# Rebuilding the routing chain between mixer and experts, and moving the mixers' scratch out of the weight slots

## The reference

```python
for l in range(DEPTH):                      # DEPTH = 2
    hn = rms_norm(x, norm_mix[l])
    mix = even_mixer(...) if l % 2 == 0 else odd_mixer(...)
    x = x + mix
    x = x + hier_moe(rms_norm(x, norm_ffn[l]), ...)
...
g_logits = xt @ w_group + b_group           # 4 groups
e_logits = xt @ w_expert + b_expert         # 32 experts
e_sel = the 8 logits of the best group;  top_v, top_i = top_k(e_sel, 2)
gate = softmax weights of the two experts * probability of the group
for each expert: acc += ge * ((silu(xt @ w1) * (xt @ w3)) @ w2)
```

## Time and profile before

| | |
|---|---|
| device time, median of 3 runs (us) | 1127.63 (1126.7 to 1129.67) |
| profiled execution: its time / its span (us) | 1127.25 / 1125.4 |
| mean granted TensorE clock | 0.956 of full speed |
| busy: PE, PEld, DVE, ACT | 76%, 48%, 32%, 23% |
| moved by DMA | 442.95 MB, mean 394 GB/s |
| layer 0: mixer and routing / experts from | 0 to 160 us / 160 us |
| layer 1: mixer and routing / experts from | 584 to 691 us / 691 us |

### The profile page before, as it was taken

The page is one execution under the profiler, slowest core; times in us unless marked ns, Lnnn a source line. Parts: engine busy times, 40 slices in busy tenths (PEclk is TensorE's granted clock), DMA queues, the critical chain, the costliest instruction groups (busy, mean ns, idle before and its releaser), DMA issues.

```text
span 1125.4 us, 25604 instructions
## 1 busy us (share of the span) xinstructions
PE 856.0 (76%) x10392; PEld 542.8 (48%) x10393; DVE 354.9 (32%) x841; ACT 262.3 (23%) x502; POOL 7.5 (1%) x16
## 2 busy tenths in 40 slices
PE   9999997777766666666689998777766666666665
...
GB/s 357 254 166 169 378 349 417 427 430 430 433 430 430 432 433 431 430 432 432 431 416 342 208 429 388 418 420 429 434 430 431 431 432 430 431 434 430 431 430 259
DMA packets 50189, 442.95 MB, mean 394 GB/s; under 512 B 4320, under 2 KB 5792, under 8 KB 23648
## 3 DMA queue, kind: packets, MB, share of 16 engines
...
q10 hardware_dynamic: 144, 0.52, 0.1%
q0 software_dynamic: 128, 0.26, 0.1%
...
## 4 chain that ended last, share of the span: by engine, by line
DMA 47%; PE 39%; DVE 6%; ACT 4%; issue 3%; SPq 1%; ACTq 0%; DVEq 0%
DMA up_pairs<-in_moe_w_dram 44%; PE low_banks L1280 13%; PE low_banks L1298 4%; PE sums_of_x L831 3%; PE sums_of_x L832 3%; PE sums_of_x L833 3%; DMA weights<-in_moe_w_dram 3%; PE low_banks L1256 2%; PE low_banks L831 1%; PE sums_of_x L1309 1%; PE low_banks L833 1%; PE low_banks L832 1%; PE low_banks L1047 1%; PE sums_of_x L1312 1%; DVE w_lo L1755 1%
## 5 line engine op out<-in xcount | busy, mean ns | idle before, releaser
L1280 PE MATMUL low_banks<-up_pairs,gates 128*32 128x256 f32 x4096 | 273.4, 426 | 117.1 <-DMA up_pairs<-in_moe_w_dram 103.4
L1280 PEld LDWEIGHTS low_banks<-up_pairs,gates 128*32 128x32 f32 x4096 | 140.7, 122 | 234.1 <-DMA up_pairs<-in_moe_w_dram 113.3
L1298 PE MATMUL low_banks<-weights,gates 128*32 128x256 f32 x2016 | 122.3, 382 | 83.0 <-DVE gates L2177 52.5
L2175 DVE TENSOR_TENSOR gates<-gates,low_banks 128x128 f32<-128x128 f32 x64 | 18.4, 287 | 389.8 <-ACT gates L1344 389.8
L1298 PEld LDWEIGHTS low_banks<-weights,gates 128*32 128x32 f32 x2016 | 62.6, 109 | 142.2 <-issue 80.8
L1344 ACT ACTIVATE gates<-low_banks 128x128 f32<-128x128 f32 x64 | 17.8, 278 | 406.4 <-PE low_banks L1280 406.4
L2171 DVE TENSOR_TENSOR gates<-low_banks,vecs 128x256 f32<-128x256 f32 x64 | 27.2, 424 | 260.6 <-PE low_banks L1265 260.6
L1256 PE MATMUL low_banks<-y_T,gates 128*32 128x256 f32 x1024 | 68.5, 385 | 13.9 <-issue 9.4
L1755 DVE TENSOR_TENSOR w_lo<-weights,w_hi 128x2048 fp32r<-128x2048 f32 x28 | 64.0, 2287 | 14.7 <-ACT w_hi L1415 14.5
L1586 ACT COPY gates<-low_banks 128x256 f32<-128x256 f32 x64 | 23.8, 372 | 191.2 <-PE low_banks L1298 191.2
L1580 ACT COPY gates<-low_banks 128x256 f32<-128x256 f32 x64 | 23.8, 372 | 158.3 <-PE low_banks L1256 158.3
...
## 6 DMA issues: line engine op xcount, KB each, us to landing
...
```

Source lines behind the costliest of these rows:

```text
L1280: ins = pe.matmul(bank[2][PASS * j:PASS * (j + 1), 0:T], got_T[:, k % 2, k // 2, :], up[:, k, :, j * P:(j + 1) * P], start=(k == 0), stop= ...
L1298: ins = pe.matmul(bank[3][PASS * q:PASS * (q + 1), T:2 * T], hid_T[:, c, :], rows_of_c[:, q * T:(q + 1) * T], start=(c == 0), stop=(c == Q ...
```

## The change

- **The last sum of x halved.** `OUT_ORDER` lists five groups instead of four: channels 0 to 255, 256 to 511, 768 to 895, 512 to 767, and last 896 to 1023. `x_added`, `mix_ready` and a new `mix_squared` count five. `OUT_BANKS` are banks 4 to 7 in both layers, and the mixer's turned outputs use `Y_BANKS`.
- **ScalarE copies sums of x.** In layer 0 ACT copies three of the four pairs of sums into the experts' banks, after squaring each. PE's `begin_sums` is left for bank 7 only. ACT also copies the logits, in place of DVE, and squares all chunks.
- **The norm.** `norms_of_mix` sums chunk 7 and the sum of the other squares in two products for each half of the tokens. ACT takes the root straight from the bank with scale and bias.
- **Turned logits** take one product for each half of the tokens, with a doubled identity (`two_of_ident`) made earlier. All four `turn(t)` come after it, in layer 1 as transposes (`is_transpose=True`).
- **Ranks in two products.** `before` times both halves at once, and `ones` times the first. The counts are read from partition 127 as rank plus `chosen`.
- **Silu's table** is asked for at the end of `route` on ACT by an activation of one column.
- **Homes packed.** The mixers' scratch leaves the `w2` part of slot 2 (it goes to `y_T`, `gates`, `tok`). In layer 0 the piece `a_g` goes through unit 0, not unit 1. So `load_down(l, 0)` and, in layer 0, `early_up(0)` (expert 2's `w3`) are issued earlier, the pieces `a_g` and `b_r` later, and `w3` of expert 0 later.

```diff
-OUT_BANKS = ((0, 2, 4, 5), (4, 5, 6, 7))
-TURN_BANKS = (6, 7, 1, 3)
-ROUTE_BANKS = ((0, 2, 4), (0, 1, 2))
+OUT_BANKS = (4, 5, 6, 7)
+OUT_ORDER = ((0, 0, 2), (1, 0, 2), (3, 0, 1), (2, 0, 2), (3, 1, 2))
+TURN_BANKS = (1, 3, 0, 2)
+ROUTE_BANKS = ((0, 2, 0), (0, 1, 2))
+RANK_BANKS = (1, 0)
+Y_BANKS = ((0, 2), (0, 1))
+ADDED = len(OUT_ORDER)
...
-    (("a_f", 0), ("a_q", 1), ("b_low", None), ("b_qk", 2), ("a_i", 3), ("b_v", 0), ("a_g", 1), ("b_r", 3),
+    (("a_f", 0), ("a_q", 1), ("b_low", None), ("b_qk", 2), ("a_i", 0), ("b_v", 3), ("a_g", 0), ("b_r", 3),
...
+        y_flat = y_T[:, :, :].rearrange("p k t -> p (k t)")
         qA, kA, bA = (work(i * 1024, 1024) for i in range(3))
-        decA = [work(3072 + i * 1024, 1024) for i in range(2)]
-        qB, kB, bB = (work(5120 + i * 512, 512) for i in range(3))
+        decA = [y_flat[:, 512:1536], work(3072, 1024)]
+        qB, kB = (work(4096 + i * 512, 512) for i in range(2))
+        bB = gates[:, 1, 512:1024]
+        decB = [y_flat[:, 1536:2048], gates[:, 0, 512:1024]]
+        SA = work(5120, 1536)
+        SB = work(6656, 1536)
         low, w_up = work(6656, T), work(6912, T)
-        masks_wide = weights[:, 2, 7168:7168 + len(LEVELS) * P]
-        SA = work(8192, 1536)
-        SB = work(9728, 1536)
-        decB = [work(11264 + i * 512, 512) for i in range(2)]
...
             def first_experts(l):
 
-                load_down(l, 0, ORDER[0])
...
-                sp_q.wait_ge(*((sums_begun, 1) if l == 0 else x_turned.at(1, 4)))
+                sp_q.wait_ge(*x_turned.at(l, 4))
+                if l == 0:
+                    sp_q.wait_ge(sums_copied, 3)
+                    sp_q.wait_ge(sums_begun, 1)
                 load_half(l, FOURTH, moe_w1, x_place, 1, fourth_up.sem)
...
             sp_q.wait_ge(*step_done.at(0, last_step(0, "a_q")))
-            piece("a_g", 1, even_w_in, C["a_g"])
+            early_up(0)
+            load_down(0, 0, ORDER[0])
             sp_q.wait_ge(*step_done.at(0, last_step(0, "b_qk")))
             load_down(0, 2, ORDER[2])
             fourth_w3(0)
             sp_q.wait_ge(*step_done.at(0, last_step(0, "a_i")))
+            piece("a_g", 0, even_w_in, C["a_g"])
+            sp_q.wait_ge(*step_done.at(0, last_step(0, "b_v")))
             piece("b_r", 3, even_w_in, C["b_r"])
-            sp_q.wait_ge(*step_done.at(0, last_step(0, "b_v")))
+            sp_q.wait_ge(*step_done.at(0, last_step(0, "a_g")))
             out_weights("even_out0", 0, even_w_out, 0)
-            sp_q.wait_ge(*step_done.at(0, last_step(0, "a_g")))
-            early_up(0)
...
                 sp_q.wait_ge(*step_done.at(0, last_step(0, "b_r") - 1 + half))
                 out_half("even_out1", 3, even_w_out, 4, half)
-                if half == 0:
-                    sp_q.wait_ge(scores_ready_B, 2 * (len(LEVELS) + 2))
-                    sp_q.wait_ge(*heads_mean.at(0, 1))
-                    load_w(0, 0, moe_w3, w3_place(0), up_loaded[up_slot(0)])
             half_down(0, 1, 0, down_loaded[ORDER[1]])
+            sp_q.wait_ge(*heads_ready.at(0, 4))
+            sp_q.wait_ge(*heads_mean.at(0, 1))
+            load_w(0, 0, moe_w3, w3_place(0), up_loaded[up_slot(0)])
...
             piece("c_g", 3, odd_w_in, C["c_g"])
+            sp_q.wait_ge(down_loaded[ORDER[(NE - 2) % 3]], down_count(0, NE - 2))
+            sp_q.wait_ge(down_done, done)
+            load_down(1, 0, ORDER[0])
             up_to(NE - 1)
             sp_q.wait_ge(*step_done.at(1, last_step(1, "d_x")))
             piece("c_v", 0, odd_w_in, C["c_v"])
...
+            def norms_of_mix(l, b):
+
+                pe.wait_ge(*mix_squared.at(l, ADDED))
+                pe.wait_ge(*logits_kept.at(l, 1))
+                for k in (7, 0):
+                    if k == 0:
+                        pe.wait_ge(*squares_added.at(2 * l, 1))
+                    for a in range(TT):
+                        ins = pe.matmul(bank[b][:, a:a + 1], squares[:, k, a * P:(a + 1) * P], const("ones", 0, 1),
+                                        start=(k == 7 and a == 0), stop=(k == 0), skip_group_check=True)
+                ins.then_inc(sums_ready.sem, 1)
+
...
+                                            start=(a == 0 and k % 2 == 0), stop=True, is_transpose=True, skip_group_check=True)
...
                 pe.wait_ge(*rest_is_set(l, i))
-                group(0)
-                group(1)
-                group(2)
-                pe.wait_ge(w_folded, 2)
-                logits_of(0)
-                logits_of(1)
-                group(3)
-                logits_of(2)
-                logits_of(3).then_inc(logits_ready.sem, 1)
-                turn(0, range(4 if l == 0 else 2))
-                norms_of_tokens(2 * l + 1, ROUTE_BANKS[l][2])
-                pe.wait_ge(*logits_kept.at(l, 1))
+                for n in range(4):
+                    group(n)
+                pe.wait_ge(w_folded, 3)
+                for n in range(3):
+                    logits_of(n)
+                group(4)
+                logits_of(3)
+                logits_of(4).then_inc(logits_ready.sem, 1)
+                norms_of_mix(l, ROUTE_BANKS[l][2])
                 for a in range(TT):
-                    for c in range(2):
-                        ins = pe.matmul(turned_logits[:, a * 64:a * 64 + ROUTE], logits_T[:, a * P:(a + 1) * P],
-                                        ident[:, 64 * c:64 * c + ROUTE], start=(c == 0), stop=(c == 1))
+                    ins = pe.matmul(turned_logits[:, a * 64:a * 64 + ROUTE], logits_T[:, a * P:(a + 1) * P], two_of_ident,
+                                    start=True, stop=True)
                 ins.then_inc(logits_turned.sem, 1)
-                if l == 1:
-                    turn(0, range(2, 4))
-                for t in (1, 2, 3):
+                for t in range(4):
                     turn(t)
...
 
-                if l == 0:
-                    begin_sums(5)
-                    pe.wait_ge(*mean_set.at(1, 1))
-                    begin_sums(4)
+                ranks = bank[RANK_BANKS[l]]
                 pe.wait_ge(*chosen_set.at(l, 1))
                 pe.wait_ge(consts_loaded, 16)
-                pe.matmul(bank[0][:, 0:NE], const("before"), chosen[:, 0, :], start=True, stop=True)
-                pe.matmul(bank[0][:, NE:2 * NE], const("before"), chosen[:, 1, :], start=True, stop=False)
-                pe.matmul(bank[0][:, NE:2 * NE], const("ones"), chosen[:, 0, :], start=False, stop=True)
-                pe.matmul(bank[0][:, 64:64 + NE], const("ones"), chosen[:, 0, :], start=True, stop=False)
-                pe.matmul(bank[0][:, 64:64 + NE], const("ones"), chosen[:, 1, :], start=False, stop=True).then_inc(ranks_ready.sem, 1)
                 if l == 0:
-                    pe.wait_ge(*x_kept.at(0, 2))
-                    begin_sums(6)
+                    pe.wait_ge(*x_kept.at(0, 1))
+                pe.matmul(ranks[:, 0:2 * NE], const("before"), chosen.rearrange("p a e -> p (a e)"), start=True, stop=True)
+                pe.matmul(ranks[:, NE:2 * NE], const("ones"), chosen[:, 0, :], start=False, stop=True,
+                          skip_group_check=True).then_inc(ranks_ready.sem, 1)
+                if l == 0:
                     begin_sums(7).then_inc(sums_begun, 1)
...
-                norm_root(2 * l + 1)
+                for n, (g, first, end) in enumerate(OUT_ORDER):
+                    act.wait_ge(*x_added.at(l, n + 1))
+                    chunks = slice(2 * g + first, 2 * g + end)
+                    f(squares[:, chunks, :], act_T[:, chunks, :], ACT.Square).then_inc(mix_squared.sem, 1)
+                    if l == 0 and end - first == 2:
+                        act.copy(pair_in_bank(OUT_BANKS[g]), pair_of(act_T, g)).then_inc(sums_copied, 1)
+                act.wait_ge(*logits_ready.at(l, 1))
+                act.copy(logits_T, bank[ROUTE_BANKS[l][0]][:, 0:T]).then_inc(logits_kept.sem, 1)
+                act.wait_ge(*sums_ready.at(2 * l, 1))
+                act.wait_ge(eps_set, 1)
+                f(root[:, :], bank[ROUTE_BANKS[l][2]][:, 0:TT], ACT.Sqrt, scale=1.0 / D, bias=eps[:, 0:1]).then_inc(rooted.sem, 1)
                 act.activation(spare[:, 1:2], zeros[:, 0:1], ACT.Exp)
...
                 keep_tokens(l, 1)
+                act.activation(spare[:, 4:5], zeros[:, 0:1], ACT.Silu)
...
-                tt(below, lm, r_tops[:, :, 0:1].to_broadcast([P, TT, NE]), ALU.subtract).then_inc(top_gap.sem, 1)
                 dve.wait_ge(vector_step, steps[0])
                 tt(chosen[:, :, :], r_left[:, :, 0:NE], lm, ALU.not_equal).then_inc(chosen_set.sem, 1)
+                tt(below, lm, r_tops[:, :, 0:1].to_broadcast([P, TT, NE]), ALU.subtract).then_inc(top_gap.sem, 1)
...
                 dve.wait_ge(*ranks_ready.at(l, 1))
-                dve.tensor_copy(counts[0:1, :], bank[0][0:1, 64:64 + NE]).then_inc(routed.sem, 1)
-                stt(place[:, :, :], bank[0][:, 0:2 * NE].rearrange("p (a e) -> p a e", a=TT), 1.0, chosen[:, :, :],
```

(3 more changed lines are left out.)

184 lines of the change are left out of this document (97 added, 87 removed).

## The result

The changed kernel takes 1130.1 us (median of 17 runs, 1127.52 to 1132.17) against 1128.48 us for the kernel before (17 runs, 1126.02 to 1130.41): ratio 1.0018, 95% interval 1.001 to 1.0025. It is slower by 1 to 3 us, within the 0.3% that I had called no change, but above my range. All ratios here are those on record, each against runs of the kernel before taken beside it (17 to 32); they differ by up to 1.1 thousandths from the quotient of the two medians (here 1.0014), and I name the medians where that changes a reading.

A forecast was written before the change was run, and what follows sets the result against it. Weight transfers fill two fixed plateaus, whose start hangs on each layer's routing up to ACT's first copy. From 1127.25 us, minus 0.8 (layer 0) and 1.7 (layer 1), plus 0.4 for the median: 1125.1 us, range 1122.5 to 1127.5.

The forecast's parts named there:

- (e): Layer 0, PE's gather: PE free by 158.1, gather starts at 159.2 instead of 160.11; gain 0.9 us.
- rival 3: PE's clock falls at the first expert, from the gather on; up to 1.7 us a layer, 1128.5 us; chance 0.09.
- (a): Layer 0, last sum and logits: sum ends as before, one chunk of logits less follows; gain 0.3 us.
- (b): Layer 0, copy of the logits: ACT copies at once, ending at 151.9 instead of 152.7 us.
- (c): Layer 0, norm and turned logits: 12 PE instructions in 1.6 us, scaling at 153.5 instead of 153.97; gain 0.5.
- (d): Layer 0, scaling to gates: no work removed, `top_gap` behind `chosen` costs 0.2 us; gates end at 158.1, gain 0.25.
- (f): Layer 0, ACT's table load moves ahead; first copy of gathered tokens at 160.45 instead of 161.25; layer gains 0.8 us.
- Rival 1: Silu's table load stands in the way of ACT reading `counts`; gains only 0.1 and 1.0, 1126.5 us; chance 0.16.
- Layer 1: Layer 1's routing: transposes take 2.1 us, first copy at 690.35 instead of 692.16; gain 1.7 us.
- The homes: Weight transfers moved earlier by packing the mixers' scratch: gains nothing by itself, but empties layer 1's queue 4.9 us earlier.
- rival 2: Transfers were the bound and packing pays: layer 1's moved 2 MB gains 4.9 us, total 1121.9 us; chance 0.10.
- Rival 4: Layer 0's mixer piece `a_g` lands late and PE stands; up to 6 us, 1131.1 us; chance 0.05.

The follow-up runs named there:

- 5: Changed kernel with the routing chain shortened at two places (sums of squares ahead of the wait for the logits' copy, `top_gap` ahead of `chosen`), no added zeros: 1.0021 of before.
- 8: Changed kernel without ACT's early table load for Silu and with `top_gap` ahead of `chosen` again: 1.0018 of before.
- 10: The shortened chain of 5 with PE kept busy by products of zeros in layer 1's routing alone: 1.0001 of before.
- kernel 11: Changed kernel with the first expert's down-weight transfers put back to the head of the first experts' loads in both layers: 1.0019 of before.
- 1: Changed kernel with products of zeros in PE's idle places of both routings, six pairs ahead of the rank products and five more behind: 1.0012 of before.
- kernel 2: Changed kernel with half the zeros of 1: layer 0 only five pairs behind the rank products, layer 1 only six ahead: 1128.64 us, one run.
- kernel 3: Changed kernel with PE's old work back: layer 0's products beginning the sums run again, layer 1's tokens turned by plain products: 1.0027 of before.
- 4: Kernel before with one part of the change alone, layer 1's tokens turned by transposes: 1.0005 of before.
- kernel 6: The shortened chain of 5 plus zeros: three pairs ahead of the rank products in both layers, behind them five in layer 0, three in layer 1: 0.9988 of before.
- 7: Kernel 6 with the first expert's down-weight transfers put back to the head of the first experts' loads in both layers: 1.0002 of before.
- 9: The shortened chain of 5 with zeros in layer 0's routing alone: 1.0001 of before.
- kernel 12: Changed kernel, chain as it is, plus zeros: three pairs ahead of the rank products in both layers, behind them five in layer 0, three in layer 1: 1.0000 of before.

## Why the prediction was wrong

The forecast was 1125.1 us, and 1130.1 was measured. The step that failed is the price of PE's removed work, which I put at nothing: (e) and the up projection behind it were costed at full clock. What happened is rival 3, "the clock falls at the first expert", to which I gave 0.09. I named its place (PE idle for 1 us and more ahead of the gather), its sign and its price (up to 1.7 a layer, 1128.5). Yet step (e) has PE "free by 158.1" and the gather at 159.2: a gap of 1.1 us, past the 1 us from which the rival was to decide, where before PE worked through (19.54 of 20 us). The forecast and the rival's own condition contradicted each other, and I didn't see it. The gather took 1.94 us and not 1.07, the up projection 4.82 and not 3.66. Layer 0 has five traces in which neither gap is covered (the changed kernel, 5, 8, 10, 11): the clock fell at the gather in four. In the nine with work in at least one gap (before, 1 to 4, 6, 7, 9, 12) it fell in none. In layer 1 it is less regular: without cover it fell between the idle time ahead of the ranks and the up projection in the changed kernel, 4, 9 and 11, and not in 5 and 8; kernel 3 is told above.

The price in layer 0 depends on when the clock comes back. 2.3 us lie between the changed kernel (Silu at 23.79) and kernel 12 (21.51): 0.9 up to the first copy, 0.2 from there to the up projection and 1.2 in it (4.82 against 3.66), and SP's next issue hangs on its first half. In kernels 5 and 11 the clock was back in time for it, and the fall cost 1.1. My 1.7 was the up projection's stretch alone.

Point by point, in us behind the first addition; up to the second idle stretch the changed kernel's clock was still full.

- (a), (b): the last half sum ends at 6.43 (6.27 before), and the logits end 0.70 behind it as before (7.13, 6.97 before), so one chunk of them less gained nothing, 0.3 forecast. That ACT copies them at once did: the copy ends at 7.54 instead of 7.98. 0.44 gained of the 0.8 forecast: the rest is this 0.3.
- (c) gave no gain, 0.5 forecast: L2157 starts at 9.30, L2119 stood at 9.26. Most of that is the missing 0.36 of (a) and (b). Behind the copy of the logits the 12 instructions took 1.76 from its end to the scaling (1.6 forecast, 1.28 in the old order). That wait was my order's own: in layer 0 the eight for the norm share bank 0 with the logits, and they need nothing else of the copy. Kernel 6, with a bank of its own and the wait behind them, has the scaling at 8.75.
- (d) was right in kind: `top_gap` behind `chosen` cost 0.28 us (4.65 us from the scaling to the end of the gates, 4.37 before), 0.2 forecast.
- (e): the gather starts at 15.26, 15.40 before: 0.14 gained of 0.9. Of the missing, 0.6 is the end of the gates (13.95, 13.4 forecast), and 0.16 that `place` still starts 0.26 behind them, as before, where I had 0.1. PE was free, as forecast, and its clock fell while it waited.
- (f) was right: the copy waited for PE, not for the table. Rival 1 is out: the load of 1.28 us at 159.67 ended at 160.95, 1.3 us ahead of the gather's end. In kernel 12, at full clock, the copy waited for PE too (0.29 us, at 161.87), and the load had ended at 161.37. A drain of 1.38 us behind it, as the Trainium skill has it ("ScalarE: Activation LUTs", "What ACT_TABLE_LOAD costs"), did not show: ACT's next instruction follows within 0.02 us.
- Layer 1: transposes 1.94 us (2.1 forecast), `place` 1.0 us earlier, gather 0.95 earlier. The first copy gained 0.15 in the changed kernel, and 1.0 in kernel 2, which kept the clock; 1.7 was forecast. What was there at the gather, the clock took back.
- The homes: no measurable gain in the changed kernel, as forecast (kernel 11); the transfers are idle for longer from 695 to 700 us (share 0.24, 0.74 before), as forecast, so rival 2 is out. Rival 4 too: ACT's rounding that hangs on `a_g` starts at 78.34 us, 77.98 before, and all roundings from 63 to 87 us are 0.36 later, so nothing waited there.

So even without the fall the change would not have reached the forecast: kernel 12's interval begins at 0.9988, and the forecast was 0.998. Of the 2.5 us the chain had 0.14 in layer 0 and 1.0 in layer 1, and 1 us is what an interval can't resolve. The Trainium skill ("TensorE: Matmul & The Clock Gate", "Part 4: PE-mode transpose") says that transposes don't count as busy for the clock as products do, and by that layer 1's fall would be theirs. Kernel 3 has plain products there and the clock fell all the same, behind 1.89 us of idle PE; kernels 5 and 8 have transposes and kept it. The runs don't tell apart what transposes add.
